# Bounding an accumulating indirect scatter by the row number in a mixture-of-experts stage

## What is computed

```python
hf = h2.reshape(512, 1024)                 # modulated, normalised x
# eidx, gw: for each token its 8 experts and their gate weights
for each block of rows (tok_b, g_b, e_b):
    xb = hf[tok_b]
    u = silu(xb @ w_gate[e_b]) * (xb @ w_up[e_b])
    y = y.at[tok_b].add((u @ w_down[e_b]) * g_b[:, None])
out = x + gt2 * rms_norm(y + shared_expert(hf), g_ffn_post)
```

## Time and profile before

| | |
|---|---|
| median of 3 runs | 1129.18 us (1128.34 to 1131.72) |
| profiled execution, its own time | 1132.51 us |
| its span, first to last instruction | 1130.7 us |
| TensorE busy | 1037.0 us, 92% |
| VectorE busy | 836.9 us, 74% |
| ScalarE busy | 521.8 us, 46% |
| POOL busy | 234.5 us, 21% |
| moved by DMA | 297.60 MB, mean 263 GB/s |
| mean granted TensorE clock | 0.972 |

### The profile page before, as it was taken

The page is one execution under the profiler, slowest core; times in us unless marked ns, Lnnn a source line. Parts: engine busy times, 40 slices in busy tenths (PEclk is TensorE's granted clock), DMA queues, the critical chain, the costliest instruction groups (busy, mean ns, idle before and its releaser), DMA issues.

```text
span 1130.7 us, 16022 instructions
## 1 busy us (share of the span) xinstructions
PE 1037.0 (92%) x4777; PEld 733.0 (65%) x4778; DVE 836.9 (74%) x1480; ACT 521.8 (46%) x610; POOL 234.5 (21%) x145
## 2 busy tenths in 40 slices
PE   1899997978998989999998999999999999899995
PEld 1898887657446447766775666667766666566662
DVE  4887899886665457787876787778787776676865
ACT  3425463364111145555554554555555454545542
POOL 0000000100000034353321323423222222342210
PEclk9899998989996999999999999999999999999998
DMA  9775300600948078999999999999999999999944
GB/s 358 244 277 178 101 1 1 229 14 13 388 186 327 27 249 269 356 344 343 338 366 348 323 333 344 345 337 329 324 338 333 346 308 339 304 328 334 340 113 152
DMA packets 82999, 297.60 MB, mean 263 GB/s; under 512 B 10799, under 2 KB 23131, under 8 KB 73437
## 3 DMA queue, kind: packets, MB, share of 16 engines
q1 hardware_dynamic: 69188, 259.12, 63.6%
q0 software_dynamic: 12208, 34.62, 13.4%
q10 hardware_dynamic: 1514, 2.97, 0.7%
HBM read 274.71 MB, written 24.12 MB: 264 GB/s over the span
## 4 chain that ended last, share of the span: by engine, by line
DMA 37%; PE 13%; issue 7%; POOLq 3%; DVE 3%; SPq 2%; ACT 1%; POOL 0%; DVEq 0%; ACTq 0%
DMA y_rows<-yb,row_numbers 28%; PE ps L2034 6%; DMA side<-in_w_exp_up 5%; PE ps L2089 4%; DMA main<-in_w_exp_up 2%; POOLq L1757 2%; DMA xg<-h_rows,row_numbers 1%; SPq L1573 1%; PE ps L2024 1%; PE ps L2134 1%; POOLq L1751 1%; ACT w_gate_up_hi L1802 1%; DVE main L2008 0%; DVE w_gate_up_lo L1901 0%; DVE pick L1881 0%
## 5 line engine op out<-in xcount | busy, mean ns | idle before, releaser
L1901 DVE TENSOR_TENSOR w_gate_up_lo<-side,w_gate_up_hi 128x2048 fp32r<-128x2048 f32 x64 | 146.8, 2294 | 78.9 <-ACT w_gate_up_hi L1802 78.8
L1901 DVE TENSOR_TENSOR w_gate_up_lo<-main,w_gate_up_hi 128x2048 fp32r<-128x2048 f32 x64 | 146.7, 2292 | 71.9 <-ACT w_gate_up_hi L1802 71.8
L1594 POOL DMA_INDIRECT y_rows<-yb,row_numbers x62 | 116.2, 1874 | 375.3 <-issue 311.4
L1802 ACT ACTIVATE w_gate_up_hi<-side 128x2048 fp32r<-128x2048 f32 x64 | 122.1, 1910 | 95.5 <-DMA side<-in_w_exp_up 54.1
L1802 ACT ACTIVATE w_gate_up_hi<-main 128x2048 fp32r<-128x2048 f32 x64 | 122.2, 1910 | 91.5 <-PE ps L2034 45.8
L2034 PE MATMUL ps<-w_gate_up_hi,xT_hi 128*128 128x512 f32 x512 | 144.7, 404 | 11.8 <-DVE xT_lo L1905 8.7
L2034 PE MATMUL ps<-w_gate_up_hi,xT_lo 128*128 128x512 f32 x512 | 137.6, 390 | 0.0
L2034 PE MATMUL ps<-w_gate_up_lo,xT_hi 128*128 128x512 f32 x512 | 137.3, 390 | 0.0
L2034 PEld LDWEIGHTS ps<-w_gate_up_hi,xT_hi 128*128 128x128 f32 x512 | 91.4, 189 | 32.1 <-issue 14.2
L2034 PEld LDWEIGHTS ps<-w_gate_up_hi,xT_lo 128*128 128x128 f32 x512 | 96.2, 188 | 21.1
L2034 PEld LDWEIGHTS ps<-w_gate_up_lo,xT_hi 128*128 128x128 f32 x512 | 96.1, 188 | 21.0
(11 more groups left out here) (309 smaller groups left out, 1554.9 us busy)
## 6 DMA issues: line engine op xcount, KB each, us to landing
side<-in_w_exp_gate SPq DMA_DIRECT2D x60, 512.0 KB, 9.6
side<-in_w_exp_up SPq DMA_DIRECT2D x60, 512.0 KB, 23.9
main<-in_w_exp_gate SPq DMA_DIRECT2D x60, 512.0 KB, 9.9
main<-in_w_exp_up SPq DMA_DIRECT2D x60, 512.0 KB, 24.6
side<-in_w_ada SPq DMA_DIRECT2D x20, 1024.0 KB, 7.7
main<-in_w_exp_down SPq DMA_DIRECT2D x16, 1024.0 KB, 23.1
maskb<-in_w_exp_down SPq DMA_DIRECT2D x16, 1024.0 KB, 20.4
side<-in_w_exp_down SPq DMA_DIRECT2D x16, 1024.0 KB, 23.6
```

The source lines that it names most:

```text
L1594: return pool.indirect_dma_start(out=G.y_sums, out_offset=bass.IndirectOffsetOnAxis(ap=sidx[0:rows, n:n + 1], axis=0), in_=yb[0:rows, slot ...
L1802: nc.scalar.activation(whi[:, half], wgu[n % RING][:, :, HALF * half:HALF * (half + 1), :] .rearrange("p m c f -> p c m f"), ACT.Copy).the ...
L1901: nc.vector.tensor_tensor(wlo[:, half], src, whi[:, half].bitcast(F32), ALU.subtract).then_inc(s_wlo, 1)
```

## The change

`add_rows` gets the bound that `gather_rows` has. Row numbers above 511 are outside it, and such rows are left out instead of being added to the spare rows:

```diff
--- before.py
+++ after.py
@@ -1592,7 +1592,8 @@
         def add_rows(pool, slot, n, rows=CAP):
 
             return pool.indirect_dma_start(out=G.y_sums, out_offset=bass.IndirectOffsetOnAxis(ap=sidx[0:rows, n:n + 1], axis=0),
-                                           in_=yb[0:rows, slot, :], in_offset=None, compute_op=ALU.add)
+                                           in_=yb[0:rows, slot, :], in_offset=None, compute_op=ALU.add,
+                                           bounds_check=SEQ - 1, oob_is_err=False)
```

## The result

| | before | after |
|---|---|---|
| median of 15 runs each | 1129.18 us | 1133.44 us |
| lowest to highest | 1124.83 to 1132.59 | 1130.98 to 1141.36 |
| ratio, 95% interval | | 1.0043 [1.0026, 1.0059] |
| profiled execution, its span | 1132.51, 1130.7 us | 1133.9, 1132.1 us |

The changed kernel is slower: the ratio says 0.43%, and the medians are 4.3 us apart. Ratios and their intervals leave out executions in a rare slow state, of which there were two in all, one of one_more_inc with 1770.74 us and one of sixteens_after with 3280.95 us. So one trace shows where things happen, but it cannot carry a difference of 4 us; that has to come from medians of changed kernels.

The account below looks back on a forecast made before the run. The prediction took DMA transfers, chiefly the weight stream, to bound the expert stage, with POOL's scatter chain close by. Skip -1.1 us and move 0 turned the median 1129.2 into 1128.1 us; range 1122.5 to 1132.6.

Parts of the forecast that it names:

- What it adds: POOL's scatter issues: one 29 ns register move each, 1.8 us over 62, taken as hidden behind the weight stream.
- The lower bound is nothing: Expert stage's scatters: the least gain is 0, since left-out rows at a transfer's end may relieve only an engine or two.
- The even relief (A): Weight stream: skipped padding relieves all 16 DMA engines evenly, saving 5.3 us, to 1123.9 us; chance 0.28.
- The block of neighbouring rows: Scatter transfers: if each engine gets neighbouring rows, skipping the last few lightens only the last engine or two.
- The reading of the gathers: Four bounded 48-row gathers landed after 8.2 us mean with rows left out, 8.1 with none: no visible gain.
- -1.1 us: Whole kernel: the gain forecast, a fifth of the even share of 5.3 us.
- The Trainium skill's rule on how a transfer is cut: DMA transfers: split over the most engines, up to 16, dividing the row count; by it the skip gains 0.
- Rival B: POOL's chain: the bounded scatter is dearer to issue, at 0.2 us each about +7 us, 1136; chance 0.12.
- Rival C: Scatters: rows past the bound still move or become empty work of equal cost; no change, 1129; chance 0.03.
- C's sum for the gathers: Software queue: moved 34.62 MB, matching 34.60 without gather padding; 264 gathered padding rows would make it 35.7.
- What would show it: Profile signs: 23.06 MB written, software queue 33.56 MB, 48-row scatters about 7.9 us, 88-row ones 10.2.
- The chain: POOL's 62 scatters in the expert stage, each waiting for the last to land: 659.7 us, without slack.

Follow-up runs that it names:

- one_more_inc: Kernel before plus one POOL semaphore increment, carried out, ahead of each scatter's branches; 1130.5 us, 1.0007 of the kernel before.
- sixteens_after: Changed kernel with issue sizes stepped by 16 rows instead of 8; 1126.4 us, 0.9968 of the kernel before.
- dead_code: Kernel before plus eleven never-executed semaphore increments per scatter tree, in the 128-row end; 1133.0 us, 1.0028 of the kernel before.
- after_again: The changed kernel, unaltered, timed and profiled a second time; 1133.4 us, 1.0039 of the kernel before.
- bound_never: Changed kernel with the bound raised to 639, so no row is skipped; 1134.6 us, 1.0040 of the kernel before.
- bound_hoisted: Changed kernel with the scatters' bound put into a register once, ahead of the loop; 1129.8 us, 1.0000 of the kernel before.
- dead_outside: Kernel before plus 88 never-executed semaphore increments behind POOL's loop; 1130.3 us, 1.0003 of the kernel before.
- leaf_wait_before: Kernel before with POOL's wait for the last scatter moved behind count reading and branches, to the issue; 1142.0 us, 1.0105 of the kernel before.
- steps of 16: Kernels with issue sizes stepped by 16 rows, not 8, giving six branch ends instead of eleven; applied to the kernel before: 1116.7 us, 0.9892.
- dead_code_40: Kernel before plus 44 never-executed semaphore increments per scatter tree, in the 128-row end; 1148.3 us, 1.0160 of the kernel before.
- leaf_wait_after: Changed kernel with POOL's wait for the last scatter moved behind the branches, to the issue; 1146.6 us, 1.0148 of the kernel before.
- both_hoisted: Changed kernel with gathers' and scatters' bounds in one register set once ahead of the loop; 1130.4 us, 1.0005 of the kernel before.
- sixteens_never: Changed kernel with sizes stepped by 16 rows and bound 639, skipping nothing; 1125.4 us, 0.9954 of the kernel before.

## Why the prediction was wrong

**The step that failed** is "What it adds": "One register move before each issue", 62 x 0.029 = 1.8 us, "I take it as hidden". For the moves that are carried out this was right: one_more_inc shows no cost. But the step counted only those, and the source's one constant had put one into each of the eleven ends of each of eight branch trees. The missing term is what instructions cost by being in POOL's loop: +88 a turn, +6 to 7 packets of instructions in the stage, +3.2 to 4.9 us (dead_code 0.28%, the change, after_again and bound_never 0.39 to 0.43%). The row that would have given it away stood on the page before, `q14 instruction: 68, 0.56`: 54 of the 68 packets fall into the 640 us in which the engines go round their loops. It wasn't read, because it has 0.1% of the engines' time.

**The bounds** followed from that. "The lower bound is nothing" excluded a loss by this edit, and the upper end of the range, 1132.6, was only the spread of measurement. With the move's own 1.8 us added to it (1134.4) the measured 1133.4 would have been inside, but by luck: the moves that are carried out are not what costs.

**The even relief (A)** was not there: bound_hoisted has the whole skip and 1.0000. Its size in engine time was well forecast, 85 us: over the kernels with these sizes the software queue's share is 13.33% on the mean where nothing is left out and 12.88% where the 258 rows are, an estimate of 0.45% x 16 x 1130 = 81 us. **The block of neighbouring rows** fits but isn't shown, as no row names an engine: expert 60's four left-out rows took 2 us of engine time and 0.2 us of landing. The reading of the gathers was right as far as it went: a row left out at the end buys nothing. The forecast's -1.1 us is within what bound_hoisted leaves open (-2.3 to +2.4 us). The Trainium skill's rule on how a transfer is cut ("DMA: Bandwidth & Descriptors", section "Why a DMA increments its semaphore by 16 and not by 1") gave 0 for the skip, and the runs agree (1.0000 [0.9980, 1.0021] in bound_hoisted).

**Rival B** had the sign, and the waits looked like it (ScalarE's wait for y_rows rose to 70.2 us), but its mechanism was not there. The issues were no dearer, the first-to-last distance was 658.8 us and not over 665, and bound_hoisted with the same bounded form lost nothing. The wait itself is no sign: one_more_inc, dead_outside and bound_hoisted, none of them slower, have 53.6 to 56.2 us of it; the kernel before with 20.3 is the one that stands out. **Rival C** was half right in a way not expected: a packet stays for each row, but a small one. The earlier trace rows had it already: a gather of 43 rows with 48 issued has 64 packets, as many as expert 60's scatter above with all its 48 rows. C's sum for the gathers was off too: their first four issues are of 128 rows, so that they have 528 rows of padding and not 264, and 36.8 MB would have been moved; it speaks against C the more.

**What would show it**: the software queue came as forecast, and so did the times of 48 and 88 rows. The written bytes did not: the page still says 24.12 MB, where 23.06 was forecast. That line can't tell a skipped row from a written one here; the software queue's can.

**The chain** read as "POOL's chain runs without slack" is true as a description, but the times don't follow from it alone, as leaf_wait_before and the steps of 16 show. Here is the piece of it between two scatters of the changed kernel, 606 to 618.6 us (start, us, what):

```profile
606.39 0.05 POOLq L1752
...
606.55 0.03 POOLq L1594
606.58 0.57 issue
...
607.40 8.42 DMA y_rows<-yb,row_numbers
615.83 0.02 issue
...
616.57 0.06 POOLq L1752
616.62 0.91 issue
617.53 0.04 POOLq L1752
...
617.77 0.03 POOLq L1594
617.80 0.57 issue
...
618.62 9.50 DMA y_rows<-yb,row_numbers
```

The move of L1594 has 0.03 us. The long parts are those in which POOL waits for nothing that the profile shows: 0.57 us after the move, which the kernel before has too (0.56 us ahead of its scatter at 636.84), and 0.91 us in the middle of the branches, where the step before had none. Summed over the 61 gaps between a landing and the next issue this is 128.0 us before and 131.1 to 133.1 in the three kernels with moves, which looks like the loss; but dead_code has 127.7 and is slower too, dead_code_40 147.7. From one profiled execution each, these sums are no proof.

**What stays open** is the way by which a longer loop costs time: stalls of POOL at branches into code that has yet to come, which shift gathers and scatters, and through them the weight stream, would fit the pieces above and the waits for weights in steps of 16. No run isolates it, and it would have to explain why the gathers' moves cost nothing. Whether another engine's loop has the same price wasn't tried.

## What to carry to other kernels

Ask of an edit inside an unrolled loop with branches how many instructions it adds to the program, not only how many are carried out: a constant operand that needs a register costs one in every branch end, and goes away when the register is set once ahead of the loop. Read the instruction queue's row; where it has packets throughout a looping stage, branch ends that are never taken are worth removing, and here this gave 0.30% where the bytes that the change saved gave nothing. Don't price rows left off the end of a transfer as their engine time over sixteen: here 258 of them shed engine time, and neither the landings nor the kernel got measurably shorter.

## What the runs showed of the hardware

- An indirect scatter's row outside the bound still has a packet, of under 512 B: 258 rows, 258 such packets more, 12208 in both.
- The page's bytes written to memory follow the rows issued, not those moved: 24.12 MB with 258 rows skipped and without; 24.90 in the kernels with steps of 16, whether 450 are skipped or none.
- Instructions of a loop are fetched anew each turn, and ones never carried out bring fetches too: 54 packets of 8 KB in the stage before, 60 with 88 dead instructions a turn, 74 with 352, 54 with 88 outside the loop. Times go with the packets across all kernels: 1116 to 1117 us at 39, 1125 to 1126 at 45 or 46, 1129 to 1131 at 53 or 54, 1133 to 1135 at 60 or 61, 1142 to 1148 at 66 to 74. Other things differ there too, and the packets are a coarse measure: leaf_wait_after has one more than leaf_wait_before and takes 4.6 us longer. The pairs above are the proof.
- Not every instruction counts alike: the gathers' 88 moves a turn taken out gave 54 to 53 packets and no time (bound_hoisted to both_hoisted).
- A scatter of more rows can land sooner: 80 rows after 8.3 us and 72 after 9.0, means of the kernel before. In seven more kernels with steps of 8 whose landings could all be read it is 8.4 to 8.9 and 8.7 to 9.5 us, the 72 rows later in each.
- The price for about the same filler depends on the kernel: 88 dead instructions cost 0.28% in steps of 8, and 48 cost 0.66% in steps of 16.
- A profiled execution may lie 4 to 6 us off its kernel's median (bound_hoisted 1124.92 against 1129.76, sixteens_never 1131.29 against 1125.41), as much as the whole effect.
